# Loads of the output block issued inside the expert loop, and pair codes kept in PSUM, in a decoder step on one core

## The reference

```
q = (x @ wq).reshape(N, 8, 2, 64)
s = einsum('thpd,hpkd->thpk', q, keys)              # 128 keys in each of two halves
sv, si = top_k(s, 16)
cand = sv[:, :, 0, :, None] + sv[:, :, 1, None, :]  # 16 x 16 pairs
cv, ci = top_k(cand, 16)
i1 = si[:, :, 0][ci // 16];  i2 = si[:, :, 1][ci % 16]
eidx = i1 * 128 + i2;        gate = softmax(cv)
h = gelu(einsum('tkd,td->tk', u_tab[eidx], x))
out = einsum('tk,tkd->td', gate * h, v_tab[eidx])
```

## Time and profile before

| | us |
|---|---|
| median of 3 runs | 2122.05 (2119.13 to 2127.99) |
| the profiled execution, its own time | 2121.11 |
| its span (first to last instruction) | 2119.2 |
| PE busy in the span | 1931.1 (91%) |
| DVE, ACT, POOL busy | 1427.9, 886.3, 768.0 |
| expert block, from barrier to barrier | 904.1 to 1553.0 |
| output block | 1553.0 to 2119.1 |

### The profile page before, as it was taken

One profiled execution on the slowest core, in us unless ns is written; L12 is line 12 of the kernel. 1 busy time (PEld: TensorE's weight loads), 2 busy tenths in 40 slices (PEclk: granted clock), 3 DMA queues, 4 the chain that ended last, 5 costly groups with the idle time before them and its releaser, 6 DMA issues. The chain is left out here.

```text
span 2119.2 us, 29569 instructions
## 1 busy us (share of the span) xinstructions
PE 1931.1 (91%) x11347; PEld 1770.1 (84%) x11347; DVE 1427.9 (67%) x2554; ACT 886.3 (42%) x1765; POOL 768.0 (36%) x438
## 2 busy tenths in 40 slices
PE   4999679877898997999998999999979999999998
PEld 3999679767896696889998999999957888777777
DVE  3686554642313214998999999955568898888885
ACT  3356212213422114334444999944433343333333
POOL 0233133222530022166775455578712132222210
PEclk9899889878999999999999999999989999999999
DMA  4232101023552313269998799999999999999993
GB/s 126 63 81 60 48 1 31 1 95 89 174 189 84 131 31 80 75 196 350 378 382 325 304 372 373 374 409 403 397 347 392 394 390 400 401 400 401 400 392 115
DMA packets 211163, 511.42 MB, mean 241 GB/s; under 512 B 13264, under 2 KB 143056, under 8 KB 174160
## 3 DMA queue, kind: packets, MB, share of 16 engines
q1 hardware_dynamic: 172720, 258.65, 35.7%
q0 software_dynamic: 27648, 201.34, 23.7%
q10 hardware_dynamic: 10656, 49.55, 5.8%
HBM read 450.48 MB, written 59.02 MB: 240 GB/s over the span
## 5 line engine op out<-in xcount | busy, mean ns | idle before, releaser
L1891 POOL TENSOR_TENSOR ex_first_ulo<-ex_first_u,ex_first_uhi 128x1024 fp32r<-128x1024 f32 x127 | 304.7, 2400 | 207.3 <-ACT ex_first_uhi L1922 103.5
L2010 PE MATMUL ps<-xhi,ex_first_uhi 128*128 128x384 f32 x1024 | 352.7, 344 | 8.2 <-PEq L1600 4.9
L2010 PE MATMUL ps<-xlo,ex_first_uhi 128*128 128x384 f32 x1024 | 344.2, 336 | 0.0
L2010 PE MATMUL ps<-xhi,ex_first_ulo 128*128 128x384 f32 x1024 | 344.1, 336 | 0.0
L1514 POOL DMA_INDIRECT ga_ring<-in_uv,ga_idx x138 | 164.0, 1189 | 310.4 <-DVE found L1540 175.4
L2309 PE MATMUL ps<-po_vhi,po_whi 128*128 128x512 f32 x768 | 240.4, 394 | 31.3 <-DVE po_wlo L2365 15.8
L2309 PE MATMUL ps<-po_vlo,po_whi 128*128 128x512 f32 x768 | 238.4, 392 | 0.0
L2309 PE MATMUL ps<-po_vhi,po_wlo 128*128 128x512 f32 x768 | 237.7, 391 | 0.0
L2010 PEld LDWEIGHTS ps<-xhi,ex_first_uhi 128*128 128x128 f32 x1024 | 193.9, 189 | 9.1 <-issue 5.1
L2309 PEld LDWEIGHTS ps<-po_vhi,po_whi 128*128 128x128 f32 x768 | 143.8, 189 | 67.8 <-issue 22.2
L2010 PEld LDWEIGHTS ps<-xlo,ex_first_uhi 128*128 128x128 f32 x1024 | 194.0, 189 | 0.0
(11 more groups left out here) (414 smaller groups left out, 4239.9 us busy)
## 6 DMA issues: line engine op xcount, KB each, us to landing
ex_first_u<-in_uT SPq DMA_DIRECT2D x128, 512.0 KB, 7.5
scores<-in_peer_v SPq DMA_DIRECT2D x32, 1024.0 KB, 9.9
po_v<-in_peer_v SPq DMA_DIRECT2D x32, 1024.0 KB, 11.9
gates<-scores ACTq DMA_DIRECT2D x12, 2048.0 KB, 12.1
scores<-gates SPq DMA_DIRECT2D x32, 768.0 KB, 15.9
acts<-ex_h ACTq DMA_DIRECT2D x62, 384.0 KB, 8.1
scores<-acts SPq DMA_DIRECT2D x31, 768.0 KB, 12.7
in_w_raw<-in_w_in SPq DMA_DIRECT2D x24, 512.0 KB, 4.0
```

Of the source, the lines that this page charges most:

```text
L1891: pool.tensor_tensor(ulo[:, j % 3], u[:, j % 3], uhi[:, j % 3].bitcast(F32), ALU.subtract).then_inc(low, 1)
L2010: mm = pe.matmul(ps[:, j % 2, 0:ND], w[:, j % 3, k, :], x[:, k, :], start=(k == 0 and n == 0), stop=(k == KT - 1 and n == 2))
```

## The change

The loads are put into SP's loop. After the load of u for j = 104 (tile 106) SP waits for the stores of the gates and loads gates 0; after j = 108 v 0; after j = 112 acts 1; after j = 116 gates 1. Nothing is left behind the loop. In select, row 2 of `code` becomes `pair_code`, 128 columns of PSUM bank 2: L2079 writes there and L2080 and L2081 read there. The number of instructions and the bytes moved are the same; `code` takes 512 bytes less in each partition.

```diff
-        code = sb("code", [P, 3, PICKS], U32)
+        code = sb("code", [P, 2, PICKS], U32)
+        pair_code = ps[:, 2, PICKS:2 * PICKS].bitcast(U32)
@@ block.sync
                     sp.dma_start(u[:, (j + 2) % 3], io["uT"][j + 2]).then_inc(u_loaded[(j + 2) % 3], 16)
-            for c in range(2):
-                sp.wait_ge(spread_stored[c], 16 * (ND // 64))
-            output.load_g(sp, io, 0)
-            sp.dma_start(output.v[:, :, :], ...).then_inc(output.v_loaded[0], 16)
-            output.load_w(sp, io, 1)
-            output.load_g(sp, io, 1)
+                if j == NKEY - 24:
+                    for c in range(2):
+                        sp.wait_ge(spread_stored[c], 16 * (ND // 64))
+                    output.load_g(sp, io, 0)
+                elif j == NKEY - 20:
+                    sp.dma_start(output.v[:, :, :], ...).then_inc(output.v_loaded[0], 16)
+                elif j == NKEY - 16:
+                    output.load_w(sp, io, 1)
+                elif j == NKEY - 12:
+                    output.load_g(sp, io, 1)
@@ select
-                after(dve.tensor_tensor(c3[:, 2], c3[:, 0], p2[:, 0].bitcast(F32), ALU.mult))
-                dve.tensor_scalar(c3[:, 0], c3[:, 2], 4, None, ALU.logical_shift_right)
-                after(dve.tensor_scalar(c3[:, 1], c3[:, 2], TOPK - 1, None, ALU.bitwise_and))
+                both = pair_code[:, 0:nj]
+                after(dve.tensor_tensor(both, c3[:, 0], p2[:, 0].bitcast(F32), ALU.mult))
+                dve.tensor_scalar(c3[:, 0], both, 4, None, ALU.logical_shift_right)
+                after(dve.tensor_scalar(c3[:, 1], both, TOPK - 1, None, ALU.bitwise_and))
```

More of the change, by code:

```diff
@@ L1876, in _ @@
                     sp.dma_start(u[:, (j + 2) % 3], io["uT"][j + 2]).then_inc(u_loaded[(j + 2) % 3], 16)
-            for c in range(2):
-                sp.wait_ge(spread_stored[c], 16 * (ND // 64))
-            output.load_g(sp, io, 0)
-            sp.dma_start(output.v[:, :, :], io["peer_v"].rearrange("(p e) d -> p e d", p=P)[:, NKEY - 4:NKEY - 2, :]
-                         ).then_inc(output.v_loaded[0], 16)
-            output.load_w(sp, io, 1)
-            output.load_g(sp, io, 1)
+                if j == NKEY - 24:
[3 more added lines that the diff above has]
+                elif j == NKEY - 20:
+                    sp.dma_start(output.v[:, :, :],
+                                 io["peer_v"].rearrange("(p e) d -> p e d", p=P)[:, NKEY - 4:NKEY - 2, :]
+                                 ).then_inc(output.v_loaded[0], 16)
+                elif j == NKEY - 16:
+                    output.load_w(sp, io, 1)
+                elif j == NKEY - 12:
+                    output.load_g(sp, io, 1)
         @block.gpsimd
```

## The result

The changed kernel takes 2131.35 us in the median of 20 runs (2124.86 to 2141.57), the kernel before 2122.99 beside it; the ratio is 1.0037, with a 95% interval of 1.0019 to 1.0055. It is 8 us slower. The prediction said 2119, 2 us faster, with a range of 2110 to 2133: the sign is wrong, though what was seen lies inside the range.

A forecast was written before the change was run, and what follows sets the result against it. No engine was taken to have room to catch up: PE sets the pace beside full transfers, so its gains or losses before 1553 move the end. -5.2 - 4.0 + 7.5 = -1.7 from 2121.1 gave 2119 us, range 2110 to 2133.

The forecast's parts named there:

- Selection, -5.2: In select, codes in PSUM free DVE from POOL, so PE resumes earlier: -5.2 us, bounds -4.6 and -6.6.
- Rival C: Selection gains nothing, as L2080 still writes SBUF and stays blocked or the stall moves to L2074: 2124.6 us, chance 0.10.
- Barrier, -4.0: Before the output block, moving 2.6 MB away lets the last gather land and POOL's drain end sooner: -4.0, bounds -2.1 and -5.8.
- Loads of u, +7.5: In the expert block, the four moved loads delay loads of u in SP's queue: +7.5 us, bounds 0 and 26.
- Tile 107: Expert block: its load of u, held behind gates 0, lands at 1453.3, so PE waits 4.1 us; latest case 11.8.
- Tile 119: Expert block: its load of u behind gates 1 lands at 1500.3 against 1499.1 needed: 1.2 us, 0 to 8.9.
- slack of 3 us: Expert block: a tile of u is ready about 3 us before PE needs it; POOL ended tile 107 3.25 us ahead.
- v 0 and acts 1: Expert block: these large loads take 2.6 us per MB at 402 GB/s, within the slack: 0.5 us for both, 0 to 2.
- Clock: Expert block: after PE's wait its clock stays lower, 5 us at 0.66, adding 1.7 us; 3.4 in the latest case.
- rival B: Starvation at both gates loads, u landing at the late ends, 25.1 us; decides from 9.2 us of waits: 2137.0, chance 0.15.
- Rival A: No starvation: gates 0's small pieces slip in and tile 107 lands by 1449; 2111.9 us, at best 2108.7, chance 0.30.

The follow-up runs named there:

- v_act: Changed kernel with v 0 and acts 1 issued from ACT's queue and both gates loads behind the last load of u; 0.9971 of the kernel before.
- v_act_shift: v_act with the gathered rows taken up four experts later in the output block; 0.9937 of the kernel before.
- gates_late: Changed kernel with gates 0 and gates 1 issued behind the last load of u, v 0 and acts 1 still ahead; 0.9991 of the kernel before.
- gates_contig: Changed kernel with both gates loads read as 6 KB rows of stored activations, same places and sizes, output not the layer's; 1.0014 of the kernel before.
- second trace: The changed kernel, unaltered, profiled once more because the first traced execution was 9 us over its median; 2132.5 us.
- gates_first: Changed kernel with gates 0 alone ahead; v 0, acts 1 and gates 1 behind the last load of u; 0.9987 of the kernel before.
- codes_only: Kernel before with only the select change, pair codes in PSUM; the four loads stay behind the last load of u; 0.9990 of the kernel before.
- four_shift: codes_only with the gathered rows taken up four experts later in the output block, four gathers still ahead of the barrier; 0.9939 of the kernel before.
- shift_only: Kernel before with only the gathered rows taken up four experts later, codes still in SBUF; 0.9989 of the kernel before.
- gates_act: Changed kernel with both gates loads issued by ACT at tiles 105 and 117, v 0 and acts 1 by SP; 1.0001 of the kernel before.
- two_shift: four_shift with two instead of four gathers of the output block issued ahead of the barrier; 0.9926 of the kernel before.

## Why the prediction was wrong

**Selection, -5.2: right.** Measured at tile 58: -4.8, and 4.5 to 6 in every pair. That ACT's softmax sets it, at 4.6, was close; PE's clock gave little more. Rival C is out: L2087 writes SBUF and is not blocked, with POOL at work beside it. Neither L2087 nor the old L2080 has a second SBUF input, so by the rule on the two sides of SBUF that the prediction quotes from the Trainium skill it must have been a two-port mode that exposed L2080. That L2080, left alone, took 0.2 us and L2087 takes 0.29 fits it; the mode itself no trace shows.

**Barrier, -4.0: the step was right, what came on top wasn't foreseen.** PE's wait shrank by 7.3 and 7.6 us, outside the bounds of -2.1 and -5.8. It has two terms. One is the time from the issue of POOL's last gather to the first matmul of the output block. Among the kernels with four gathers ahead of the barrier it is 19.1 to 21.0 us in the five with 2.6 MB behind the last load of u (20.1 before); with only the two gates loads there, 1.5 MB, 17.4 or 17.5 (v_act, v_act_shift, gates_late); with none 15.3 to 16.1 in seven traces. Its 4.5 to 4.8 us are the 4.0 of the prediction. Its ground holds as well: the last gather landed 7.8 us after its issue instead of 12.3, and the drain ended 4.4 us behind the landing, where it was 4.3 before. The other term is how long before PE's last tile that gather is issued: 4.4 us before (1540.24 less 1535.89) and 7.1 in the changed kernel (1559.46 less 1552.32). Of the 7.3 us these 2.8 were won because PE itself was late, and are paid for in the loop. In gates_contig, where it is 4.2 us again, the wait is 11.2 us, 4.6 less than before.

**Loads of u, +7.5: the step that failed.** It was mis-sized by a factor of two and a half or more, and with it the sign of the whole was wrong. Measured +19.0 and +21.9, within the bounds of 0 and 26. Its parts:

- Tile 107: a landing 18.0 us after the issue of the gates was forecast, 10.5 of hold and 7.5 to land. It was 20.1 in both traces (1456.0 less 1435.87, 1446.3 less 1426.20). In the first the hold ended 12.35 us after the issue of the gates (1448.22 less 1435.87), near the 13.0 of the earlier trace rows; in the second 8.6, less than the 10.5 of the earlier trace rows, and u landed no sooner. So the forecast split the time where it doesn't split: hold and landing make up one sum. The wait was 6.4 us, 6.0 in the second trace, instead of 4.1.
- Tile 119: this is the term that failed, 1.2 us forecast and 8.6 measured. The forecast let gates 1 be issued at 1482.3 and PE start tile 119 at 1502.6, 20.3 us on. In the trace they are 1494.62 and 1511.22 (1519.84 less the wait), 16.6 us. PE had been put off by its own wait, but SP by more, since v 0 and acts 1 had pushed the loads of u back and POOL's slack was down to 0.1 to 0.8 us at tiles 115 to 118. That is half of the miss, 3.7 us. I counted each of the four loads against the full slack of 3 us, as if it came back within four tiles. In gates_first, without the two large loads, the slack at tile 119 was 3.5 us. The other half is again the time from the gates to the landing of u, 21.7 us (1516.3 less 1494.62) instead of 18. In the second trace, where PE had waited at tile 111 already, the wait was 7.2 us.
- v 0 and acts 1: 0.5 us forecast from 1 MB at the full 402 GB/s. But a load in SP's queue didn't have the full rate: they cost 6.8 us in gates_late, and u landed 15.9 us after its issue behind v 0. In the first trace they show as slack that is gone, in the second as a wait of 2.6 us besides.
- Clock: 1.7 us forecast for one wait, 4.0 measured for two.
- The slack of 3 us itself came from one trace. In four traces without early loads (before, codes_only, four_shift, shift_only) it lies between 0.05 and 4.1 us at tiles 106 to 127.

With 15.05 us of waits the case was rival B's, which was to decide from 9.2. Its 2137 less the 3.3 us that the barrier gave beyond its term is 2134, 2 us over what was measured, in part by luck, as it put 25 us on the loads of u. With the measured terms, -4.8 + 19.0 - 7.3 = +6.9, and -5.0 + 21.9 - 7.6 = +9.3 in the second trace, the difference of the medians of 8.4 is accounted for within the scatter.

**Rival A is out**, and the holds that the prediction set against it were seen. The Trainium skill, DMA: Bandwidth & Descriptors, section "Specifications", gives 512 bytes as enough for line rate. Here two loads of 768 KB cost 7.5 to 10.4 us more in 512-byte pieces than in 6 KB rows by the traces, 5 us by the ratios, and the next issue was held for 5 to 9 us instead of 0.3; the measurement decides.

## What to carry to other kernels

A load put in front of a stream that an engine lives on costs what it takes from that stream's slack, and the next one starts from what is left: add up the loads over the stretch, not each against the full slack. Behind a load of many small pieces, take as its price the time from its issue to the landing of the next load, in the busiest stretch of the trace; the time for which the issue is held varies and is not that price. Take the slack from more than one trace. Where a barrier waits for the drain of gathers, the bytes moved out of it and the waits taken out of it came back elsewhere while the transfers were full; what helped was to take up the gathered rows later behind the barrier.

## What the runs showed of the hardware

- SP's issue of u behind a transfer in 1536 pieces of 512 bytes was held for 9.2 and 8.9 us in one trace of the changed kernel, 5.5 and 5.3 in the other and 5.6 in gates_first. Behind the same bytes in 128 rows of 6 KB it took 0.328 us (gates_contig). ACT's store behind such a transfer was held for 12.7 us once and once not at all (gates_act). The hold stays with the queue: within ACT's hold SP issued a load of u at 1446.6 in 0.33 us.
- With a hold of 9.2, 5.5 or 5.6 us, u landed 17 us after SP had come to its issue; with 6 KB rows ahead of it, 11.2 us.
- PE's granted clock was 0.53 and 0.61 in windows of 7 and 13 us that take in the ends of waits of 6.4 and 8.6 us and what follows them, and PE lost 4 us beside the 15 of waiting.
- POOL's drain ended 16.6 us after the issue of its last gather before (1552.5 less 1535.9), 12.2 in the changed kernel (1564.5 less 1552.3). It ended 4.3 or 4.4 us behind the landing of that gather in seven traces. Two gathers fewer moved its end from 12.9 us behind PE's last matmul (codes_only) to 1.2 (two_shift).
- A DVE instruction from SBUF to SBUF (L2080) took up to 2.44 us beside POOL's subtraction, and with its input in PSUM (L2087) never more than 0.293.
